# Up projections of a two-block transformer kernel: order of the low weights' products, two row blocks at a time

## The reference, cut to what matters

```python
# first block
hn = rmsnorm(h, norm2_g[layer])
a = jnp.square(jax.nn.relu(hn @ w_ff1[layer]))        # w_ff1: 1024 x 4096
h = h + a @ w_ff2[layer]
# layers 0 and 1 of the second block
g, u = split_cols(h @ w_in, [D_FF_2, D_FF_2])         # ffn_w_in: 1024 x 5632, D_FF_2 = 2816
return (jax.nn.silu(g) * u) @ w_out
```

## Time and profile before

| | |
|---|---|
| median of three executions | 1042.93 us |
| the profiled execution | 1043.34 us, of it 1041.6 us from the first to the last instruction (the span) |
| PE, matmuls | busy 1035.2 us (99%), 6408 matmuls |
| PE, weight loads | busy 912.6 us (88%), 6408 loads |
| VectorE, ScalarE, GpSimd | busy 729.1, 594.8 and 57.3 us |
| mean DMA rate | 177 GB/s |

### The profile page before, as it was taken

The page is one execution under the profiler, slowest core; times in us unless marked ns, Lnnn a source line. Parts: engine busy times, 40 slices in busy tenths (PEclk is TensorE's granted clock), DMA queues, the critical chain, the costliest instruction groups (busy, mean ns, idle before and its releaser), DMA issues.

```text
span 1041.6 us, 15854 instructions
## 1 busy us (share of the span) xinstructions
PE 1035.2 (99%) x6408; PEld 912.6 (88%) x6408; DVE 729.1 (70%) x857; ACT 594.8 (57%) x751; POOL 57.3 (6%) x53
## 2 busy tenths in 40 slices
PE   9999999999999999999999999999999999999998
PEld 8998999888888889888888888889998888888887
DVE  6888887676565567965766666677989676666665
ACT  6677545554444456765644444476777664444464
POOL 0000001200000030002006000010000200000010
PEclk9999999999999999999999999999999999999999
DMA  9636354645646546445456555455424455455641
GB/s 323 214 122 202 123 192 136 207 174 190 214 162 205 199 142 202 123 178 180 162 199 208 186 192 200 163 188 177 163 81 162 132 202 202 163 205 185 213 165 41
DMA packets 129192, 184.28 MB, mean 177 GB/s; under 512 B 3296, under 2 KB 103008, under 8 KB 129120
## 3 DMA queue, kind: packets, MB, share of 16 engines
q1 hardware_dynamic: 128672, 182.68, 52.2%
q0 software_dynamic: 160, 0.52, 0.2%
q10 hardware_dynamic: 288, 0.07, 0.0%
HBM read 182.21 MB, written 1.05 MB: 176 GB/s over the span
## 4 chain that ended last, share of the span: by engine, by line
PE 99%; DMA 1%; SPq 0%; DVE 0%; ACT 0%; issue 0%
PE PS L410 96%; PE PS L418 2%; DMA H<-in_x_dram 1%; SPq L2738 0%; SPq L2742 0%; DVE O L2577 0%; ACT O L1746 0%; ACT AR L1666 0%; DVE AR L2445 0%; DVE H L2447 0%
## 5 line engine op out<-in xcount | busy, mean ns | idle before, releaser
L1847 DVE TENSOR_TENSOR WL<-RAW,WH 128x2048 fp32r<-128x2048 f32 (+1 forms) x171 | 370.8, 2174 | 114.0 <-ACT WH L1234 113.5
L1234 ACT ACTIVATE WH<-RAW 128x2048 fp32r<-128x2048 f32 (+1 forms) x180 | 326.9, 1820 | 84.3 <-PE PS L410 75.6
L410 PE MATMUL PS<-WH,X 128*128 128x512 f32 (+1 forms) x1104 | 302.7, 355 | 0.0
L410 PE MATMUL PS<-O,WH 128*128 128x512 f32 (+1 forms) x880 | 239.1, 361 | 0.0
L410 PEld LDWEIGHTS PS<-WH,X 128*128 128x128 f32 x1104 | 195.8, 189 | 29.8 <-issue 1.9
L410 PE MATMUL PS<-X,WH 128*128 128x256 f32 (+1 forms) x864 | 202.0, 330 | 0.0
L410 PE MATMUL PS<-WL,X 128*128 128x512 f32 (+1 forms) x552 | 194.6, 353 | 0.0
L410 PEld LDWEIGHTS PS<-O,WL 128*128 128x128 f32 x744 | 134.6, 189 | 22.8
L410 PE MATMUL PS<-O,WL 128*128 128x256 f32 x744 | 153.2, 281 | 0.0
L410 PE MATMUL PS<-WH,O 128*128 128x512 f32 (+1 forms) x464 | 141.0, 378 | 0.1
L410 PEld LDWEIGHTS PS<-O,WH 128*128 128x128 f32 x880 | 137.7, 190 | 3.3 <-issue 0.3
(11 more groups left out here) (219 smaller groups left out, 782.4 us busy)
## 6 DMA issues: line engine op xcount, KB each, us to landing
RAW<-in_ffn_w_in_dram SPq DMA_DIRECT2D x44, 1024.0 KB, 5.1
RAW<-in_w_ff_dram SPq DMA_DIRECT2D x32, 1024.0 KB, 5.3
RAW<-in_ffn_w_out_dram SPq DMA_DIRECT2D x22, 1024.0 KB, 5.0
RAW<-in_w_in_dram SPq DMA_DIRECT2D x19, 1024.0 KB, 5.2
RAW<-in_gla_w_in_dram SPq DMA_DIRECT2D x12, 1024.0 KB, 5.4
RAW<-in_diff_w_in_dram SPq DMA_DIRECT2D x12, 1024.0 KB, 5.1
RAW<-in_ple_w_gate_dram SPq DMA_DIRECT2D x8, 1024.0 KB, 5.0
RAW<-in_w_out_dram SPq DMA_DIRECT2D x4, 1024.0 KB, 5.1
```

Of the source, the lines that this page charges most:

```text
L410: return e.matmul(o, l, r, start=start, stop=stop, skip_group_check=skip)
L1234: act(high, raw, ACT.Copy).then_inc(s["w_hi"], 1)
L1847: e.tensor_tensor(low, raw, high.bitcast(F32), ALU.subtract).then_inc(s["w_lo"], 1)
```

## The change

In `feat_wide` the calls with a `norm` keep their order. In the others the narrow matmuls of two row blocks come together: first the wide ones of the first block, then the narrow ones of blocks 0 and 1, the wide ones of blocks 1 and 2, the narrow ones of blocks 2 and 3, and so on, and at the end the wide ones of block 7. The count of matmuls, their shapes, operands and banks stay the same. (The wide ones now pass `skip_group_check`, which is no part of the instruction's work.)

```diff
-        for k in ks:
-            if norm:
+        def wides(k):
+            for fb in range(2):
+                i = mm(PS[:, bank + fb, :], w[0][:, k, fb * 128:fb * 128 + 128], m.both(ops, k), k == 0, k == 7, True)
+            return i
+
+        def narrows(k):
+            for fb in range(2):
+                mm(PS[:, bank + fb, 0:256], w[1][:, k, fb * 128:fb * 128 + 128], high[:, k, :], False, False, True)
+
+        if norm:
+            for k in ks:
                 ahead(norm, k)
...
+        else:
+            wides(ks[0])
+            for k in ks[1::2]:
+                narrows(k - 1)
+                narrows(k)
+                i = wides(k)
+                if k < ks[-1]:
+                    wides(k + 1)
```

More of the change, by code:

```diff
@@ L497, in feat_wide @@
             ready(c)
-        for k in ks:
-            if norm:
-                ahead(norm, k)
[L501 to L509, removed]
+        def wides(k):
[7 more added lines that the diff above has]
+            for k in ks:
+                ahead(norm, k)
+                if k:
+                    narrows(k)
+                i = wides(k)
+                if k == 0:
+                    narrows(k)
+        else:
+            wides(ks[0])
+            for k in ks[1::2]:
+                narrows(k - 1)
+                narrows(k)
+                i = wides(k)
+                if k < ks[-1]:
+                    wides(k + 1)
         if ks[-1] == 7:
```

## The result

The changed kernel takes 1045.08 us in the median of 12 runs (1044.55 to 1046.25), against 1042.97 us (1042.49 to 1043.4) for the kernel before in 12 runs beside it: ratio 1.0021, 95% interval 1.0013 to 1.0029. Timed once more on another occasion it was 1.0018 (1.0009 to 1.0027). So the change costs about 2.1 us where the forecast had 1.4. The time lies inside the range given for 8 in 10 (1042.2 to 1045.7 us), but at the upper edge of the narrower band that the forecast itself was given (+0.5 to +2.1 us, 1043.4 to 1045.0 us): 1045.08 us is just above it.

The account below looks back on a forecast made before the run. PE's own matmul stream was taken to bound the kernel; 57 chunks x 3 merged pairs x 8 ns gave +1.4 us, so 1044.3 us in the median, with 1042.2 to 1045.7 us for 8 in 10.

Parts of the forecast that it names:

- PE never waits there: Up chunks: PE does not wait, so none of the added 1.4 us lies beside other work.
- merged pair of periods: Up chunks: two periods of two narrow, two wide become four wide, four narrow; 1.40 against 1.392 us, +8 ns, 171 times.
- row at 530.51: Earlier trace, part 0 to part 1: four wide 0.93 us, four narrow 0.47, together 1.40; the row the forecast used.
- row at 210.07: Earlier trace: four wide in 0.92 us, giving 1.39 with four narrow, -2 ns each, -0.3 us, 1042.6 us in all.
- The head and the end as before: Full chunk: head (two wide, four narrow) and end (two wide) were taken as unchanged, leaving three pairs that cost +8 ns.
- Worth nothing: Rival on up chunks: the order has no price, as loads under narrow matmuls stay as many; 1042.6 to 1042.9 us; chance 0.28.
- Fewer changes of width: Faster rival, up chunks: half the width changes, wide ones reach steady pace, four under 0.91 us; down to 1040.5 us; chance 0.06.
- Bound by its loads: Slower rival, middle narrow runs of 57 chunks: loads fall behind, 0.120 us or more each; 1045.1 to 1046.3 us; chance 0.14.
- 1.405 us: Cost of four wide plus four narrow from which the slower rival decides, 13 ns above now, 2.09 us over 171.
- The rule of the Trainium skill: Matmul distance is columns over 2.4 plus about 2.5 ns (109 ns for 256, 216 for 512), so the order changes 0.

Follow-up runs that it names:

- runs of sixteen: Changed kernel with all sixteen narrow matmuls of an up chunk in one run, before block 7's wide ones; 1042.05 us, ratio 0.9992; timed again 1041.72 us, 0.9985.
- the mix: Changed kernel with runs of unequal length: two wide, then repeatedly four narrow, two wide, two narrow, four wide, ending four narrow, two wide; 1042.55 us, ratio 0.9997.
- two runs of eight: Changed kernel with an up chunk's narrow matmuls in two runs of eight, behind the wide ones of blocks 3 and 6; 1042.65 us, ratio 1.0001.
- one by one: Changed kernel with single narrow and wide matmuls alternating from block 1 on, for each column half (block 0 wide, narrow); 1044.83 us, ratio 1.0016.

## Why the prediction was right, and what it missed

- **PE's stream is the bound and has no slack.** Right: the waits of PE are the same two groups, the clock is full, and the time moved by what the stream moved. "PE never waits there" fails in one of 57 chunks, the one before 216.24, where a stop of some 0.2 us that the list of waits leaves out swallowed the chunk's 0.03 us.
- **The price of a merged pair of periods, +8 ns.** Right: 1.403 against 1.392 in the timeline shown, 10 ns by the medians (929 + 474 against 2 x 696.5). Four wide at 0.93 and four narrow at 0.47 were forecast and are there. In the up chunks this gives the forecast's 1.4 us. But the choice of the row was in part luck. The row at 530.51 was taken "since it has both runs and the narrow ones ahead", and the row at 210.07, which gave 1.39 us and no loss, has all of that too: both stand behind a narrow pair, not behind four, and both have four narrow behind them. They differ in the narrow pair ahead, 232 ns at 530.51 and 228 at 210.07. (The 0.22 and 0.24 us of two pairs, averaged as rounding, were in part these two kinds.)
- **"The head and the end as before", and the down projections at 0.227 us.** Wrong, and it is the third of the loss that was missed: 37 places x 0.020 = 0.7 us (35 down projections, and the `ple_w_proj` product behind the first pair of each layer). The four matmuls at the end of a chunk were priced by the earlier trace rows, behind a narrow pair, though in the changed kernel they stand behind four narrow ones at the end of a chain of fours. I had read in that row that the slow pace runs on into the down projection, and did not ask what a longer chain leaves there. Before, its first three matmuls take 228, 233 and 231 ns, and then 227; in the changed kernel the first seven stand at 236, 224, 231, 236, 228, 233 and 231. With it the sum is 2.1 to 2.2 us, and the measured difference is 2.1.
- **The reason for the price.** The prediction left open whether narrow runs (0.120 in a long run) or wide runs were at fault. The runs of sixteen show that long narrow runs are harmless, and the mix shows that runs of four are harmless beside runs of two. It is the wide matmuls behind a narrow run that are slow for five places, 0.02 us net in all, and a pattern of four and four pays nearly all of it every time and hands some on. Two and two pays 3 ns a run: the chunk before has seven narrow runs and takes 5.575 us, 0.020 more than the one with a single run.
- **The rivals.** "Worth nothing" is excluded by the interval (1.0013 and above). "Fewer changes of width" had four wide at 0.91 or less; in the changed kernel they are not. With one narrow run in a chunk it comes true: that is where the better kernel was, on the far side of the change, while two runs of eight only equal the kernel before. "Bound by its loads" had the right sign and nearly the right time, for half the reason: it expected 0.48 in the narrow runs, and they stand at 0.470 and 0.478 by turns (474 ns in the mean). A merged pair stayed under its 1.405 us, and the time passed 1045.0 only with the down projections.
- **The rule of the Trainium skill** (TensorE: Matmul & The Clock Gate, section Back-to-back issue gap) gives a distance by the columns alone. Taken for the same distance whatever the neighbours, it fails in both directions: the order is worth +2.1 us one way and -0.8 to -1.2 us the other.

Still open: what in the chip makes the debt, and what sets how long it runs on. The distances show that a run begun in the middle of a debt goes differently from one begun at the steady pace, but "forgiven when the next narrow run starts" gave the right number for the mix and the wrong one for one by one, so it is no more than a description. Four and four leaves a longer tail (5.472 against 5.452), one by one a longer one still in the first network (5.489) and less in the layers (5.463), and a short stop of PE leaves one in the kernel before, at 216.24, with no run of four and four ahead. So the longer tail does not belong to the new order alone. Nor was the order of sixteen tried across the two parts of a pair, which would hold a chunk's slot longer.

## What to carry to other kernels

Where one engine's stream is the whole time, an order of unequal matmuls has a price of its own, and it is read from the distances between starts, not from durations or counts: look up each run length with the runs ahead of it and behind it, look for more than one place, since the same neighbours can have two prices (917 and 930 ns here), and follow the last run into the stage that comes next. Either keep the short matmuls in few long runs, or check in the trace that the pattern in use is one of the cheap ones. Fewer switches are not better step by step: from seven narrow runs in a chunk to four it got worse, to two the same as before, to one better.

## What was not expected of the hardware

- Matmuls of 512 columns behind a run of narrow ones stand at 233, 236, 228, 233 and 231 ns before they are back at 227, the same behind 8 and 16 narrow ones.
- In the first network one chunk of 16 wide and 16 narrow matmuls takes 5.555 us with one narrow run, 5.569 with runs of 4, 2, 4, 2, 4, 5.575 with two of eight or with one of four and six of two, 5.602 with four of four, and 5.631 one by one: 0.076 us, 1.4%, between orders of the same work.
- The same order can go at two paces: one by one, a narrow and a wide take 353 ns in part 0 of a pair and 347 in part 1; four wide behind two narrow take 917 or 930 ns.
- The two banks' order and a jump of 8 KB within the moving operand change nothing, to about a nanosecond a matmul.
- With 128 columns the distances in a run are 110 to 113 ns after the first, not half of the 120 with 256 columns.
